# Strassen's seven half-block products for the two feed-forward input products of a two-block fp32 network

## What is computed

```python
gu = h @ w_ffn_in[l]
f = jax.nn.silu(gu[..., :D_FF]) * gu[..., D_FF:]
x = x + _rmsnorm(f @ w_ffn_out[l], g_ffn_post[l])
...
ff = conv_ffn(h, ffn_w_up[l], ffn_conv_w[l], ffn_conv_b[l], ffn_w_down[l])
h = layer_norm(ALPHA * h + ff, ln_g[l, 2], ln_b[l, 2])
```

## Time and profile before

| | us |
|---|---|
| median of three runs | 4441.47 |
| lowest and highest run | 4441.04, 4446.75 |
| the profiled execution | 4455.6 |
| its span, first to last instruction | 4453.8 |
| TensorE matmuls busy in the span | 4173.4 (94%) |
| TensorE weight loads busy | 3580.8 (80%) |
| VectorE busy | 1117.2 (25%) |
| ScalarE busy | 539.9 (12%) |

### The profile page before, as it was taken

One profiled execution on the slowest core, in us unless ns is written; L12 is line 12 of the kernel. 1 busy time (PEld: TensorE's weight loads), 2 busy tenths in 40 slices (PEclk: granted clock), 3 DMA queues, 4 the chain that ended last, 5 costly groups with the idle time before them and its releaser, 6 DMA issues.

```text
span 4453.8 us, 48379 instructions
## 1 busy us (share of the span) xinstructions
PE 4173.4 (94%) x20932; PEld 3580.8 (80%) x20932; DVE 1117.2 (25%) x2168; ACT 539.9 (12%) x1093; POOL 160.2 (4%) x294
## 2 busy tenths in 40 slices
PE   8999979999998989999999998988897999999997
PEld 7788868888886878888888887866486788888886
DVE  1444476771222010000000024721401222221001
ACT  0333301111111010000000000221302100000001
POOL 0000000001110000000000000010000000000000
PEclk9999989999999999999999999996898999999998
DMA  6555544436443433444455554451132344443562
GB/s 230 193 207 212 200 151 170 164 135 220 180 157 131 147 119 142 154 154 153 151 202 213 217 184 163 147 181 18 16 122 100 109 154 154 154 151 146 214 224 96
DMA packets 84963, 705.69 MB, mean 158 GB/s; under 512 B 19392, under 2 KB 19472, under 8 KB 46240
## 3 DMA queue, kind: packets, MB, share of 16 engines
q1 hardware_dynamic: 39888, 580.93, 35.4%
q0 software_dynamic: 20800, 75.43, 5.4%
q10 hardware_dynamic: 24112, 46.97, 2.9%
HBM read 652.10 MB, written 51.18 MB: 158 GB/s over the span
## 4 chain that ended last, share of the span: by engine, by line
PE 89%; DVE 5%; ACT 2%; DMA 2%; issue 1%; ACTq 1%; DVEq 0%; POOL 0%; POOLq 0%
PE product_bank L352 52%; PE product_bank L374 24%; PE mixer_bank L943 2%; DVE yT L863 1%; PE mixer_bank L491 1%; DVE arena L866 1%; PE mixer_bank L503 1%; DMA units<-out_stage 1%; PE mixer_bank L963 0%; DVE arena L1057 0%; PE mixer_bank L831 0%; PE mixer_bank L1789 0%; PE product_bank L1819 0%; PE mixer_bank L1765 0%; PE mixer_bank L1761 0%
## 5 line engine op out<-in xcount | busy, mean ns | idle before, releaser
L352 PE MATMUL product_bank<-hT,weight_ring 128*128 128x256 f32 x4096 | 891.2, 380 | 10.6 <-DVE hT L546 8.5
L352 PEld LDWEIGHTS product_bank<-hT,weight_ring 128*128 128x128 f32 x4096 | 780.7, 191 | 118.9 <-issue 9.2
L374 PE MATMUL product_bank<-hT,weight_ring 128*128 128x256 f32 x3584 | 804.0, 383 | 0.0
L374 PEld LDWEIGHTS product_bank<-hT,weight_ring 128*128 128x128 f32 x3584 | 683.3, 192 | 102.7 <-issue 8.9
L352 PE MATMUL product_bank<-xT,weight_ring 128*128 128x256 f32 x3072 | 668.3, 381 | 11.7 <-ACT xT L572 11.7
L352 PEld LDWEIGHTS product_bank<-xT,weight_ring 128*128 128x128 f32 x3072 | 586.8, 191 | 93.0 <-issue 12.4
L352 PE MATMUL product_bank<-arena,weight_ring 128*128 128x256 f32 x2944 | 640.1, 380 | 7.9 <-DVEq L2091 5.2
L352 PEld LDWEIGHTS product_bank<-arena,weight_ring 128*128 128x128 f32 x2944 | 560.1, 190 | 85.7 <-DVEq L2091 5.6
L374 PE MATMUL product_bank<-xT,weight_ring 128*128 128x256 f32 x768 | 171.3, 380 | 0.8 <-PE mixer_bank L1552 0.3
L1325 DVE TENSOR_TENSOR arena<-arena,product_bank 128x256 f32 (+1 forms) x44 | 18.5, 421 | 587.6 <-ACT arena L1310 587.6
L374 PEld LDWEIGHTS product_bank<-xT,weight_ring 128*128 128x128 f32 x768 | 145.6, 190 | 22.1 <-issue 2.2
(11 more groups left out here) (448 smaller groups left out, 2987.1 us busy)
## 6 DMA issues: line engine op xcount, KB each, us to landing
weight_ring<-in_weights SPq DMA_DIRECT2D x277, 2048.0 KB, 7.8
units<-out_stage ACTq DMA_DIRECT2D x91, 256.0 KB, 7.9
rwkv_keep<-arena ACTq DMA_DIRECT2D x16, 1282.0 KB, 7.2
arena<-rwkv_keep POOLq DMA_DIRECT2D x8, 2048.0 KB, 10.2
arena<-units POOLq DMA_DIRECT2D x62, 256.0 KB, 3.8
arena<-units POOLq DMA_DIRECT2D x60, 128.0 KB, 6.1
arena<-in_rw_pack POOLq DMA_DIRECT2D x16, 261.0 KB, 6.2
arena<-rwkv_keep POOLq DMA_DIRECT2D x4, 1024.0 KB, 7.5
```

The costliest lines, as they stand in the source:

```text
L352: mm = pe.matmul(out, lhs, rhs, start=first, stop=kk == slots * st.blocks - 1, skip_group_check=slots > 1)
L374: mm = pe.matmul(psg[b][:, half * T:half * T + T], lhs, rhs, start=k == 0, stop=k == 15)
```

## The change

The unit of "ffn_in" and of "up2" stays 256 output features, but is computed as a product of 2 x 2 blocks: tokens in two halves of 128, output features in two halves, and the contraction in even and odd blocks. Strassen's scheme in Winograd's form needs seven products of half-blocks instead of eight. Each of the seven is eight fp32 matmuls with a 128x128 weight and 128 token columns. Four combinations S1 to S4 of the source are made once a stage on VectorE (into yT for the first stage, into hT for the second). Three sums of weights and one in place in the ring slot are made per unit on VectorE, two units ahead, into two buffers in turn. Each unit now accumulates in four quarters of two banks (X and Y), and the pairs of banks alternate. When a unit is done, VectorE recombines them in five operations, with one product copied out by ScalarE first, since an operation reads at most one bank.

The three operations on each unit follow on: in "ffn_in" the silu on ScalarE and the product on VectorE; in "up2" the first tap moves from VectorE to ScalarE (two Identity activations with scale and bias), VectorE keeps two taps, and the product of unit u-1 is done after the recombination of unit u. The stages that follow wait for the blocks of each slot (parts) in place of the whole stage, and their first two units wait for the last two recombinations. All loops of both stages are written out. The sums of units 0 and 1 of "ffn_in" stand on VectorE ahead of the norm after "out"; the sum of unit 0 of "up2" ahead of its wait for the layer norm. The norm scratch of mix_post and ffn_pre moves to column 0 of the arena.

```diff
+                if isinstance(i, int) and i == 0 and j < 2 and st.bank in SEVENS_END:
+                    pe.wait_ge(bank_free[(b + 2) % 4], (st.bank + j - 2) // 4 + 1)
                 for n in range(slots):
+                    if parts and isinstance(i, int) and i == j == 0:
+                        pe.wait_ge(sem(parts), st.blocks * (n + 1))
...
+        def combine_source_dve(dve, name, src, into):
+
+            A11, A12, A21, A22 = source_blocks(src)
+            S1, S3, S2, S4 = combined_source(into)
+            done = sem(f"{name}_source_combined")
+            dve.tensor_tensor(S1, A21, A22, ALU.subtract).then_inc(done, 1)
+            dve.tensor_tensor(S3, A11, A21, ALU.subtract).then_inc(done, 1)
+            dve.drain()
+            dve.tensor_tensor(S2, S1, A11, ALU.subtract).then_inc(done, 1)
+            dve.drain()
+            dve.scalar_tensor_tensor(S4, S2, -1.0, A12, ALU.mult, ALU.subtract).then_inc(done, 1)
+
+        def sum_weights_dve(dve, name, u, into):
+
+            pos = UNIT_AT[name, u][0]
+            B11, B12, B21, B22 = weight_blocks(pos)
+            s1, s2, s4 = sums_of(into)
+            if u >= 2:
+                dve.wait_ge(w_used, UNIT_AT[name, u - 2][0] + 1)
+            dve.wait_ge(w_ready[pos % RING], 16 * (pos // RING + 1))
+            dve.tensor_tensor(s1, B11, B12, ALU.add)
+            dve.drain()
+            dve.tensor_tensor(s2, s1, B22, ALU.add)
+            dve.tensor_tensor(B12, B12, B22, ALU.add)
+            dve.drain()
+            dve.tensor_tensor(s4, s2, B21, ALU.add).then_inc(sem(f"{name}_weights_summed"), 1)
+
+        def unit_sevens(pe, name, u, src, sums, combined, ready=None, count=0):
...
+            else:
+                pe.wait_ge(bank_free[(seq - 2) % 4], (seq - 2) // 4 + 1)
+            pe.wait_ge(w_ready[pos % RING], 16 * (pos // RING + 1))
+            pe.wait_ge(sem(f"{name}_weights_summed"), u + 1)
...
+            for n, (bank, at, lhs, rhs) in enumerate([
+                    (Y, 2, B11, A11), (Y, 0, s4, A22), (Y, 1, s1, S1),
+                    (X, 0, B21, A12), (X, 3, B12, S3), (X, 1, s2, S2), (X, 2, B22, S4)]):
+                if u == 0 and n in (2, 4, 5, 6):
+                    pe.wait_ge(got, {2: 1, 4: 2, 5: 3, 6: 4}[n])
+                for j in range(DB // 2):
+                    if ready and n == 0 and j % 2 == 0:
+                        pe.wait_ge(sem(ready), count - NCK + 1 + j // 2)
+                    mm = pe.matmul(bank[:, at * P:at * P + P], lhs[:, j, :], rhs[:, j, :], start=n in (0, 3) and j == 0,
+                                   stop=j == DB // 2 - 1, skip_group_check=True)
...
+        def recombine_dve(dve, name, u, first, u2, t_u3, left, right):
...
+            dve.wait_ge(w_used, pos + 1)
+            dve.wait_ge(sem(f"{name}_first_copied"), u + 1)
+            dve.tensor_tensor(u2, X[:, P:2 * P], first, ALU.add)
+            dve.tensor_tensor(left[:, 0:P], X[:, 0:P], first, ALU.add)
+            dve.drain()
+            dve.tensor_tensor(halves(t_u3), halves(X[:, 2 * P:4 * P]), twice(u2), ALU.add)
+            dve.drain()
+            dve.tensor_tensor(left[:, P:2 * P], t_u3[:, P:2 * P], Y[:, 0:P], ALU.add).then_inc(sem(f"{name}_left"), 1)
+            dve.tensor_tensor(halves(right), twice(Y[:, P:2 * P]), halves(t_u3), ALU.subtract)\
+                .then_inc(bank_free[seq % 4], 1)
...
         def ffn_dve(dve):
...
+            dve.drain()
+            combine_source_dve(dve, "ffn_in", hT, yT)
+            for u in range(st.units):
+                left, right, first, u2 = ffn_out_of[u % 2]
+                recombine_dve(dve, "ffn_in", u, first, u2, ffn_t, left, right)
+                if u + 2 < st.units:
+                    sum_weights_dve(dve, "ffn_in", u + 2, ffn_sums[u % 2])
+                dve.wait_ge(sem("ffn_silu"), u + 1)
+                dve.drain()
+                dve.tensor_tensor(fT[:, u, :], left, right, ALU.mult).then_inc(sem("ffn_mul"), 1)
...
         def conv_dve(dve):
             st = PLAN["up2"]
+            sum_weights_dve(dve, "up2", 0, up_sums[0])
             dve.wait_ge(sem("ln_done"), 2 * NCK)
+            combine_source_dve(dve, "up2", xT, hT)
+            sum_weights_dve(dve, "up2", 1, up_sums[1])
...
+            for u in range(st.units):
+                col = lambda h, k: cv_p[:, 8 * u + 4 * h + k:8 * u + 4 * h + k + 1]
+                U, V = cvu[:, u % 4, :, :], cvt[:, u % 2, :, :]
+                recombine_dve(dve, "up2", u, up_first[u % 2], up_u2, up_t, U[:, 0, 2:258], U[:, 1, 2:258])
+                if u:
+                    product(u - 1)
+                if u + 2 < st.units:
+                    sum_weights_dve(dve, "up2", u + 2, up_sums[u % 2])
+                dve.drain()
+                dve.wait_ge(sem("conv_first_tap"), u + 1)
+                for k in (1, 0):
+                    for h in range(2):
+                        last = dve.scalar_tensor_tensor(V[:, h, :], U[:, h, k:k + T], col(h, k), V[:, h, :], ALU.mult, ALU.add)
+                    dve.drain()
+                dve.nop().then_inc(sem("conv_done"), 1)
+            product(st.units - 1)
```

More of the change, by code:

```diff
@@ L317, in wait, with products @@
                 eng.wait_ge(s, value)
-        def products(pe, name, src, ready=None, count=1, chunks=1, after=None):
+        def products(pe, name, src, ready=None, count=1, chunks=1, after=None, parts=None):
             st = PLAN[name]
@@ L358, in products, with pair_of, weight_blocks @@
             groups(pe, st, peel=chunks > 1 or after is not None)(unit)
+        SEVENS = ("ffn_in", "up2")
+        SEVENS_END = [PLAN[n].bank + PLAN[n].units for n in SEVENS]
+        def pair_of(name, u):
+            end = PLAN[name].bank + PLAN[name].units
+            pair = (1 - end % 4 // 2 + PLAN[name].units - 1 - u) % 2
+            return psg[2 * pair], psg[2 * pair + 1]
+        def weight_blocks(pos):
+            w = ring[:, pos % RING, :].rearrange("p (j two n) -> p j two n", two=2, n=256)
+            return w[:, :, 0, 0:P], w[:, :, 0, P:2 * P], w[:, :, 1, 0:P], w[:, :, 1, P:2 * P]
@@ L1298, in build @@
         fT = arena[:, 0:FB * T].rearrange("p (b t) -> p b t", b=FB)
-        silu = carve(4 * T, at=16384)[0].rearrange("p (s t) -> p s t", s=4)
-        def ffn_act(act):
[L1302 to L1315, removed]
+        FB_AT = FB * T
@@ new lines, in build, with ffn_pe @@
+        ffn_sums = [arena[:, FB_AT + 3072 * n:FB_AT + 3072 * n + 3072] for n in range(2)]
+        ffn_out_of = [carve(T, T, P, P, at=FB_AT + 6144 + n * 768) for n in range(2)]
+        ffn_t = carve(T, at=FB_AT + 6144 + 2 * 768)[0]
+        def ffn_pe(pe):
+            for u in range(PLAN["ffn_in"].units):
+                run(unit_sevens(pe, "ffn_in", u, hT, ffn_sums[u % 2], yT, ready=None if u else "ffn_in", count=NCK))
+        def ffn_act(act):
+            for u in range(PLAN["ffn_in"].units):
+                left, right, first, u2 = ffn_out_of[u % 2]
+                if u >= 2:
+                    act.wait_ge(bank_free[UNIT_AT["ffn_in", u - 2][1] % 4], UNIT_AT["ffn_in", u - 2][1] // 4 + 1)
+                copy_first_act(act, "ffn_in", u, first)
+                act.wait_ge(sem("ffn_in_left"), u + 1)
+                act.activation(left, left, ACT.Silu).then_inc(sem("ffn_silu"), 1)
@@ L1317, in ffn_dve, with ffn_sums_dve @@
+        def ffn_sums_dve(dve):
+            for u in range(2):
+                sum_weights_dve(dve, "ffn_in", u, ffn_sums[u])
         def ffn_dve(dve):
             st = PLAN["ffn_in"]
[L1320 to L1333, removed]
+            dve.drain()
+            combine_source_dve(dve, "ffn_in", hT, yT)
+            for u in range(st.units):
+                left, right, first, u2 = ffn_out_of[u % 2]
+                recombine_dve(dve, "ffn_in", u, first, u2, ffn_t, left, right)
[4 more added lines that the diff above has]
+                dve.tensor_tensor(fT[:, u, :], left, right, ALU.mult).then_inc(sem("ffn_mul"), 1)
@@ L2037, in conv_pool, with up_pe @@
             pool.dma_start(cv_p, t_in["conv"]).then_inc(sem("conv_in"), 16)
+        up_sums = [carve(3072, at=15616)[0], yT.rearrange("p b t -> p (b t)")[:, 0:3072]]
+        up_first = carve(P, P, at=18688)
+        up_u2, up_t = carve(P, T, at=18944)
+        def up_pe(pe):
+            for u in range(PLAN["up2"].units):
+                run(unit_sevens(pe, "up2", u, xT, up_sums[u % 2], hT, ready=None if u else "ln_done", count=2 * NCK))
         def conv_act(act):
-            st = PLAN["up2"]
@@ L2202, in _ @@
             gates_act(act)
-            scaled_into_y(act, "out", "g_mix_post")
+            scaled_into_y(act, "out", "g_mix_post", "mix_post")
             root_act(act, "mix_post", pm[0], 0)
```

125 lines of the change are left out of this document (67 added, 58 removed).

## The result

The changed kernel takes 4330.2 us in the median of four runs (4327.2 to 4330.4), against 4443.4 for the kernel before (four runs, 4441.0 to 4446.8): a ratio of 0.9743 with a 95% interval of 0.9726 to 0.9760, or 113 us less. 4331 us and 110 us less were forecast.

What follows compares the result with a forecast made beforehand. TensorE's number and pace of matmul instructions was taken as the bound. -109 + 2.2 + 4.6 - 1.4 - 5.2 - 1.6 = -110.4 us, taken as -110 from the 4441.47 us median, gave 4331 us; range 4297 to 4363 us.

Steps and rivals of the forecast that it cites:

- Units: In both stages, 112 pairs of 112 ns make a unit 12.54 us against 13.81; 109 us less over 86 units.
- bound of 109 ns: Lower bound for a load and matmul pair in both stages, if fixed costs stay hidden; 29 us less.
- Start of the first stage: In ffn_in, the first product needs all 16 blocks of hT, plus a half-clock stretch; unit 0 ends 2.2 us later.
- half-level stretch: At each stage's start, TensorE works for a time at half clock after standing nearly idle; 1.85 us added.
- Start of the second: In up2, unit 0 waits for VectorE's weight sums, 4.9 us after its last scaling, plus half clock; 4.6 us later.
- Ends: Out products no longer wait for the last unit's evaluation, and a half-clock stretch goes; gains 1.4, 5.2 and 1.6 us.
- VectorE's cover: VectorE's work per unit, at most 7.4 us in ffn_in and 9.5 in up2, stays hidden beside TensorE's 12.5 us.
- Weight loads, fetch of unrolled code: In both stages, weights arrive in time and instruction fetch keeps up: zero cost; upper bound for fetch gaps 29 us.
- Rival A: In up2, VectorE's strided sums take twice 1.22 us and set the unit at 14.4 us; 4413 us, chance 0.07.
- Rival B: In all 88 units, loads are not hidden behind matmuls, a unit takes 24.0 us; about 5320 us, chance 0.04.
- extra 25 ns a pair: Skill page's estimate for 128-column pairs, not adopted: 134 ns a pair, a unit of 15.0 us, about 100 us lost.
- Rival C: TensorE stands once a unit for sums or banks, giving back the 109 us; about 4440 us, chance 0.02.

Runs made afterwards that it cites:

- e1: The kernel before, with each matmul of the two stages cut into two of 128 token columns, eight half-block products and no scheme; 4497.5 us.
- e7: The changed kernel with 64-column weights in the seven products, matmuls still streaming 128 columns, result not computed; 4304.0 us.
- e10: e6 plus matmuls into an unused bank while TensorE waits ahead of and inside the first product of both stages; 4324.4 us.
- e6: The changed kernel with the weight sums of up2's unit 0 made ahead of the layer norm's reciprocal; 4327.1 us.
- e5: The changed kernel with the waits of both out products put back to the whole stage, all 44 blocks; 4344.1 us.
- e4: The changed kernel with two more additions, each with a drain, in each unit's weight sums on VectorE; 4332.0 us.
- e3: The changed kernel with four more additions, each with a drain, in each unit's weight sums on VectorE; 4428.3 us.
- e8: The changed kernel with 64 token columns in each of the seven products' matmuls, loads still 128 x 128, result not computed; 5327.7 us.
- e9: e3 with ScalarE's copy of the next unit's first product moved ahead of the Gelu in up2; 4407.3 us.

## Why the prediction was right

The forecast was 110 us less, the medians gave 113. The terms as measured in the traces, -112 + 2.2 + 4.9 - 1.4 - 5.2 - 1.6, are -113.

- **Units**, -109 us forecast: 2 x 43 x (13.81 - 12.51) = -112. The 112 ns were 111.7, and 111.7 again in e1 with another kernel around them. The bound of 109 ns is what a pair costs when its load is half as long (e7). Taking 112 ns for 111.7 made the 3 us. That the pair's last 2.6 ns come from the two sides being equal was argued in the forecast and is not shown by any run.
- **Start of the first stage**, +2.2 us: 19.82 - 17.59 = +2.2. The half-level stretch that was added for a start of this kind, at 1.85 us, is there; e10, with the clock kept up, has 1.9 us less.
- **Start of the second**, +4.6: 24.32 - 19.43 = +4.9. VectorE's sums stand ahead of TensorE's start as worked out (3420.23 to 3425.2, 4.9 us). But the split between the sums and the clock was only argued: taking the sums out of this place (e6) gave 1.6 us back, and e10 with the clock at 1.00 another 1.9.
- **Ends**, -1.4, -5.2 and -1.6: both waits are gone, and down2's products are 1.6 us shorter (309.3 against 310.9). The profiled executions then lose 1.7 us again in the last norm, which takes another time in other traces of the same code. The reverse (e5) costs 12.0 us, where these and the longer chain behind a unit gave 9.7; in its trace the clock's part is 2.8 us for 1.6.
- **VectorE's cover**, at most 7.4 and 9.5 us of 12.5: it is busy 6.6 and 8.3 us a unit (282.5 and 358.1 us over 43), and e4 shows that 2.6 us more are free. What the text did not see is that its period is not only its own work. In e3, where VectorE is the slowest, the ring through ScalarE's Gelu and copy adds 0.75 us to its wait in each unit.
- **Weight loads, fetch of unrolled code**, zero: TensorE has no gap in 538 us of either stage, at 169 and 165 GB/s against 167 forecast.
- **Rival A** (VectorE sets up2): refuted by e4; a sum reads strided blocks of the ring in 1.22 us, as from plain buffers.
- **Rival B** (loads not hidden, about 5320 us): refuted for this kernel, pairs of full rows overlap at 111.7 ns over 88 units. The rule of the Trainium skill, TensorE: Matmul & The Clock Gate, section What overlaps and what doesn't, that loads overlap running matmuls only in other row groups, does not hold for these pairs. Nor does the extra 25 ns a pair, which was an estimate from its section Back-to-back issue gap. In e8 the time of rival B came about (5328 us), by another mechanism, the clock.
- **Rival C** (TensorE stands once a unit): there is no such wait.

The profiled execution was forecast at 4345 us and came out at 4330.2, 15 us lower. The spans differ by 125 us, but 14.6 us of this lie in the unchanged stages between ffn_out and up2's norm. The gain taken from the medians does not hold this part. The forecast's lowest time, 4297 us, is 2 us above what its own terms give (4331 - 29 - 6.8); nothing rests on it.

## What to carry to other kernels

Where a matmul and its weight load are equally long, take the price of the pair from a row with the same balance, as the 64-column pairs here gave 112 ns for a measured 111.7. A scheme that trades columns for loads paid here with the columns as long as the load; with the columns at half the load's length (e8) the kernel was far slower. Count the slack of a helping engine round the whole ring of waits that passes through it, not by its busy time. Compare medians of runs, not two profiled spans, when a stage between has a clock that comes and goes.

## What the runs showed of the hardware that was not expected

- With 64-column matmuls behind 128-column loads (e8), the granted clock stayed at 0.50 through both stages, over 1000 us each (1055 us in ffn_in), with TensorE busy all the time; with 128-column matmuls behind 64-column loads (e7) it was 1.00. With half the streamed columns the kernel took 5328 us and not 4330.
- The weight load follows TensorE's clock: 213 ns for 128 fp32 columns at the half level in e8.
- TensorE had a gap once a unit in e3 (50.0 us over 34 units, the longest 2.4) and in e9 (52.7 us over 35, the longest 1.8). The clock of the window was 0.96 in e3 and 1.00 in e9; why it fell only in e3 stays open.
- Matmuls into an unused bank during waits kept the clock at 1.00 at both starts of e10, where it was 0.50 without them. This saved 1.9 us at each start.
- The same 32 matmuls of the last norm took 7.17, 8.8 to 8.9 or 10.15 us, by the trace, in code that no edit touched.
